# Modulation rows summed four at a time, 32 partitions each, from one accumulator tile

## The reference

```
silu_c, silu_cc = silu(c), silu(c_ctx)
for i in range(2):                                    # first block
    m  = (silu_c  @ w_mod[i] + b_mod[i]).reshape(9, 1024)    # w_mod[i]: 1024 x 9216
    mc = (silu_cc @ w_mod[i] + b_mod[i])                     # layer 0 only
    x = x + 0.5 * m[2] * swiglu(rms_norm(x) * (1 + m[1]) + m[0]);  cs likewise with mc
    x = x + m[5] * mixer(rms_norm(x) * (1 + m[4]) + m[3])
    x = x + 0.5 * m[8] * swiglu(rms_norm(x) * (1 + m[7]) + m[6])
for i in range(2):                                    # second block, conditioned on c_2
    mod = (silu(c_2) @ ada_w[i] + ada_b[i]).reshape(6, 1024)
    ...                                               # mixer and 16 experts, modulated by mod
```

## Time and profile before

| | us |
|---|---|
| median of 3 runs | 2507.69 |
| lowest and highest run | 2500.26, 2511.84 |
| the profiled execution | 2501.64 |
| its span, first to last instruction | 2499.8 |
| PE busy (share) | 2397.4 (96%) |
| DVE busy | 1430.5 (57%) |
| ACT busy | 1000.5 (40%) |
| DMA: bytes, mean rate | 535.45 MB, 214 GB/s |

### The profile page before, as it was taken

One profiled execution on the slowest core, in us unless ns is written; L12 is line 12 of the kernel. 1 busy time (PEld: TensorE's weight loads), 2 busy tenths in 40 slices (PEclk: granted clock), 3 DMA queues, 4 the chain that ended last, 5 costly groups with the idle time before them and its releaser, 6 DMA issues.

```text
span 2499.8 us, 35746 instructions
## 1 busy us (share of the span) xinstructions
PE 2397.4 (96%) x15358; PEld 2158.7 (86%) x15358; DVE 1430.5 (57%) x1609; ACT 1000.5 (40%) x1257; POOL 4.5 (0%) x12
## 2 busy tenths in 40 slices
PE   9999999989999999999999988899999899899997
PEld 7788888867998999888998986899998888899996
DVE  0875676323763465234652442688887433888886
ACT  2211132214330332042321323577776344676774
POOL 0000000000000000000000000000000000000000
PEclk8999999989999999999999988899999789899998
DMA  7456767522777477543775431488886332488884
GB/s 277 172 196 240 265 227 271 192 68 79 259 279 277 171 292 294 186 152 129 262 276 212 151 118 37 148 300 294 300 305 242 142 121 75 179 304 295 296 307 180
DMA packets 94195, 535.45 MB, mean 214 GB/s; under 512 B 9984, under 2 KB 12296, under 8 KB 46800
## 3 DMA queue, kind: packets, MB, share of 16 engines
q1 hardware_dynamic: 92480, 524.33, 58.3%
q0 software_dynamic: 816, 5.65, 0.6%
q10 hardware_dynamic: 736, 3.10, 0.3%
HBM read 531.97 MB, written 1.06 MB: 213 GB/s over the span
## 4 chain that ended last, share of the span: by engine, by line
PE 90%; DVE 6%; ACT 3%; issue 1%; DVEq 0%; ACTq 0%
PE PS L777 25%; PE PS L1231 12%; PE PS L850 9%; PE PS L888 8%; PE PS L1259 7%; PE PS L812 5%; PE PS L935 5%; DVE moe_low L2202 2%; PE PS L1199 2%; PE PS L733 2%; PE PS L699 2%; PE PS L1179 1%; PE PS L659 1%; PE PS L742 1%; PE PS L876 1%
## 5 line engine op out<-in xcount | busy, mean ns | idle before, releaser
L777 PE MATMUL PS<-h_parts,ring_low 128*128 128x256 f32 (+1 forms) x1408 | 440.0, 313 | 0.0
L777 PE MATMUL PS<-h_parts,g_parts 128*128 128x256 f32 x2112 | 383.0, 284 | 0.9 <-DVE h_parts L1813 0.9
L2202 DVE TENSOR_TENSOR moe_low<-moe_ring,W_HIGH 128x2048 fp32r<-128x2048 f32 x128 | 292.9, 2290 | 83.1 <-ACT W_HIGH L1615 83.1
L777 PEld LDWEIGHTS PS<-h_parts,g_parts 128*128 128x128 f32 x2112 | 328.9, 192 | 2.4 <-issue 1.2
L1231 PE MATMUL PS<-moe_low,HXH 128*96 128x256 f32 x1024 | 287.9, 281 | 0.0
L777 PEld LDWEIGHTS PS<-h_parts,ring_low 128*128 128x128 f32 x1408 | 269.9, 192 | 16.1
L1615 ACT ACTIVATE W_HIGH<-moe_ring 128x2048 fp32r<-128x2048 f32 x128 | 244.5, 1912 | 23.4 <-PE PS L1259 22.7
L850 PE MATMUL PS<-G,ring 128*128 128x256 f32 x1056 | 236.5, 385 | 2.8 <-DVE G L1898 2.8
L850 PEld LDWEIGHTS PS<-G,ring 128*128 128x128 f32 x1056 | 201.3, 192 | 30.7 <-DVE G L1898 3.4
L1460 ACT ACTIVATE SG<-PS 128x256 f32<-128x256 f32 (+1 forms) x88 | 38.4, 437 | 462.9 <-PE PS L777 462.9
L1231 PEld LDWEIGHTS PS<-moe_low,HXH 128*96 128x96 f32 x1024 | 166.2, 162 | 0.3
(11 more groups left out here) (316 smaller groups left out, 4653.6 us busy)
## 6 DMA issues: line engine op xcount, KB each, us to landing
moe_ring<-moe_w SPq DMA_DIRECT2D x192, 1024.0 KB, 4.9
CB<-mod_rows SPq DMA_DIRECT2D x200, 512.0 KB, 5.9
ring<-up_w SPq DMA_DIRECT2D x88, 1024.0 KB, 5.0
ring<-lin_w SPq DMA_DIRECT2D x55, 1024.0 KB, 4.9
ring<-down_w SPq DMA_DIRECT2D x24, 1408.0 KB, 6.0
CB<-mod_dual SPq DMA_DIRECT2D x24, 512.0 KB, 4.1
ring<-down_w SPq DMA_DIRECT2D x10, 1024.0 KB, 7.8
ring<-mod_w SPq DMA_DIRECT2D x8, 1024.0 KB, 7.0
```

Of the source, the lines that this page charges most:

```text
L777: return mm(dst(h), a[:, k, h * P:(h + 1) * P], b[:, k, :], start=start, stop=(k == KT - 1 and j == 2), skip_group_check=True)
L2202: tt(by_tile(moe_low[:, moe_slot(l, p), :]), by_tile(moe_ring[:, moe_slot(l, p), :]), w_high_tiles(p), ALU.subtract).then_inc(w_low, 1)
```

## The change

The sums of four rows are made from one accumulator. A **group** is four consecutive rows (7 groups for 28 rows). Each row keeps 32 of the accumulator's partitions: chunk m of a group (m = 0 to 31) holds, of each of its four rows, the 32 contraction indices m*32 to m*32 + 31, so 4 x 32 partitions by 1024 outputs, 512 KB as before. The number of chunks stays at 224, and so do DVE's instructions for a chunk, but the doubled ones are 32 now instead of 24, since the first group has four rows. The moving tile of the sums becomes a 128 x 4 table of ones and zeros (`block`), so each product gives four columns, written 8 columns apart in PSUM.

`chunk_in` issues one load a chunk whose source is `[4 rows][32 indices][1024]`, the rows 4 MB apart in DRAM; for the first group two loads, `[3][32][1024]` into 96 partitions and `[1][32][1024]` into 32. There is one accumulator for groups 1 to 6, in roots. The table of chunks, the banks and the waits (`rows_taken`, `mods_ready`) follow the groups. The conditions must be laid out by 32 partitions: POOL loads them with four small loads at the start, ACT waits for these (`ld_cond`) and takes one silu of 128 x 128. The host's data is the same. The diff, cut to its core:

```diff
+ROWS, PARTS = 4, 32
+GROUP_CHUNKS = KT * P // PARTS
+N_GROUPS = (N_DUAL + N_ROWS) // ROWS
+def group_cond(g):
+    return 0 if g < 4 else 2
 CHUNKS_AT = (
-    ([3] * 8 + [4] * 9 + [3] * 4 + [0], [4] * 5 + [2] + [4, 2] + [4] * 3 + [0]),
-    ([1, 1, 2] * 6 + [1, 1, 0, 0], [3, 2, 3, 2, 2, 2, 0, 0]),
-    ([1, 1, 2] * 6 + [1, 1, 0, 0], [3, 2, 3, 2, 2, 2, 0, 0]),
-    ([1] * 20 + [0, 0], [2] * 6 + [0, 0]),
+    ([3] * 10 + [2] + [4] * 8 + [0, 4, 0], [4] * 5 + [2, 4, 2, 0, 4, 4, 0]),
+    ([1, 1, 2] * 6 + [0, 1, 1, 0], [3, 3, 2, 2, 2, 2, 0, 0]),
+    ([2, 1] * 5 + [1, 0] + [1, 2] * 4 + [1, 0], [2] * 5 + [1, 0, 0]),
+    ([1] * 8 + [0] + [1, 2] * 6 + [0], [3, 3, 2, 2, 2, 2, 0, 0]),
 )
+GROUP_BANK = (6, 4, 7) + (4,) * (N_GROUPS - 3)
...
-                if n % KT == KT - 1:
-                    r, at = n // KT - N_DUAL, min(i + 1, len(counts) - 2)
...
+                if n % GROUP_CHUNKS == GROUP_CHUNKS - 1:
+                    steps[i + 1]["sums"].append(n // GROUP_CHUNKS)
+                    steps[i + 2]["takes"].append(n // GROUP_CHUNKS)
...
+def rows_landed(n):
+    return 16 * (n // 4 + 1 + min(n // 4 + 1, GROUP_CHUNKS // 4))
...
+    t["block"] = (i[:, None] // PARTS == np.arange(8)[None, :])
...
             def chunk_in(n):
-                src = mod_dual[n] if n < N_DUAL_CHUNKS else mod_rows[n - N_DUAL_CHUNKS]
+                g, k, part = n // GROUP_CHUNKS, n % GROUP_CHUNKS // ROWS, slice(n % ROWS * PARTS, (n % ROWS + 1) * PARTS)
                 if n >= 4:
                     sp.wait_ge(acc_steps, steps_after(n - 4))
-                sp.dma_start(ROWS_W[:, n % 4, :], src).then_inc(rows_full[n % 4], 16)
+                def put(j, rows, src):
+                    dst = ROWS_W[j * PARTS:(j + rows) * PARTS, n % 4, :]
+                    sp.dma_start(dst, src).then_inc(rows_full[n % 4], 16)
+                if g == 0:
+                    put(0, N_DUAL, mod_dual[k::KT, part, :])
+                    put(N_DUAL, 1, mod_rows[k:k + 1, part, :])
+                else:
+                    r0 = ROWS * (g - 1) + 1
+                    put(0, ROWS, mod_rows[r0 * KT + k:(r0 + ROWS - 1) * KT + k + 1:KT, part, :])
...
-            def column_sums(r):
-                pe.wait_ge(acc_steps, steps_after((N_DUAL + r + 1) * KT - 1))
...
-                for d in range(KT):
-                    last = mm(PS[:, ROW_BANK[r], d:d + 1], ACC[ROW_ACC[r]][:, d * P:(d + 1) * P], tab("ones")[:, 0:1],
-                              start=True, stop=True)
+            def column_sums(g):
+                pe.wait_ge(acc_steps, steps_after((g + 1) * GROUP_CHUNKS - 1))
+                wait(pe, rows_taken, g)
+                for j in range(1 if g else 2):
+                    acc = ACC if g else DUAL_ACC[:, j, :]
+                    for d in range(KT):
+                        at = j * ROWS * KT + d
+                        last = mm(PS[:, GROUP_BANK[g], at:at + 3 * KT + 1:KT], acc[:, d * P:(d + 1) * P],
+                                  tab("block")[:, 0:ROWS], start=True, stop=True)
                 last.then_inc(colsum_done, 1)
-            def dual_column_sums(r):
...
@@ down0 on PE
-                            pe.wait_ge(rows_taken, 11)
+                            pe.wait_ge(rows_taken, 3)
...
@@ ACT at the start
+            act.wait_ge(ld_cond, 64)
+            af(cond_rows[:, :, :], cond_raw[:, :, :], ACT.Silu).then_inc(cond_ready, 1)
...
@@ POOL at the start
+            for part in range(ROWS):
+                src = bass.AP(cols_in.tensor, part * PARTS * NCOLS, [[0, ROWS], [NCOLS, PARTS], [1, 4 * KT]])
+                pool.dma_start(cond_raw[:, part, :], src).then_inc(ld_cond, 16)
...
             def add_chunk(n):
+                g, m = n // GROUP_CHUNKS, n % GROUP_CHUNKS
+                dve.wait_ge(rows_full[n % 4], rows_landed(n))
+                for j in range(1 if g else 2):
+                    acc = ACC if g else DUAL_ACC[:, j, :]
+                    at = 4 * (m // ROWS) + (group_cond(g) if g else j)
+                    c = cond_rows[:, m % ROWS, at:at + 1]
+                    if m == 0:
+                        if g > 1:
+                            dve.wait_ge(colsum_done, g)
+                        ts(acc, w, c, None, ALU.mult).then_inc(acc_steps, 1)
+                    else:
+                        dve.wait_ge(acc_steps, steps_after(n - 1) if g else 2 * n - 1 + j)
+                        stt(out=acc, in0=w, scalar=c, in1=acc, op0=ALU.mult, op1=ALU.add).then_inc(acc_steps, 1)
```

More of the change, by code:

```diff
@@ L84, in chunk_plan @@
         counts = list(ups_at) + list(downs_at)
-        steps = [dict(chunks=[], sums=[], dual=[], takes=[]) for _ in counts]
+        steps = [dict(chunks=[], sums=[], takes=[]) for _ in counts]
         for i, count in enumerate(counts):
@@ L88, in chunk_plan @@
                 steps[i]["chunks"].append(n)
-                if n % KT == KT - 1:
-                    r, at = n // KT - N_DUAL, min(i + 1, len(counts) - 2)
-                    if r < 0:
-                        steps[at]["dual"].append(r + N_DUAL)
-                    else:
-                        steps[at]["sums"].append(r)
-                        steps[min(at + 1, len(counts) - 1)]["takes"].append(r)
+                if n % GROUP_CHUNKS == GROUP_CHUNKS - 1:
+                    steps[i + 1]["sums"].append(n // GROUP_CHUNKS)
+                    steps[i + 2]["takes"].append(n // GROUP_CHUNKS)
                 n += 1
         plan.append(steps)
-    assert n == (N_DUAL + N_ROWS) * KT
+    assert n == N_GROUPS * GROUP_CHUNKS
     return plan
@@ L157 @@
 _TABS = (("ident", P), ("flip", P), ("mean64", P), ("mean128", P), ("mean1024", P), ("rot_axial", P),
[L158 removed]
+         ("rot_half", P), ("upper", P), ("ones", P), ("zeros", P), ("w4", 8), ("w16", 32), ("iota", CAP), ("block", 8),
          ("cos_axial", S), ("sin_axial", S), ("cos_half", S), ("sin_half", S),
@@ L690, in first_mods @@
                 spread_roots(0)
[L692 to L711 removed]
+            def column_sums(g):
[7 more added lines that the diff above has]
+                                  tab("block")[:, 0:ROWS], start=True, stop=True)
+                last.then_inc(colsum_done, 1)
             def sums(f, i):
[L715 to L718 removed]
+                for g in PLAN[f][i]["sums"]:
+                    column_sums(g)
             def h_arrived(n, k):
@@ L1870, in add_chunk @@
-                r, k = q // KT, q % KT
-                c, acc = cond_flat[:, q:q + 1], ACC[ROW_ACC[r]]
-                if k == 0:
-                    wait(dve, colsum_done, max([0] + [o + 1 for o in range(r) if ROW_ACC[o] == ROW_ACC[r]]))
-                    ts(acc, w, c, None, ALU.mult).then_inc(acc_steps, 1)
-                else:
-                    dve.wait_ge(acc_steps, steps_after(n - 1))
-                    stt(out=acc, in0=w, scalar=c, in1=acc, op0=ALU.mult, op1=ALU.add).then_inc(acc_steps, 1)
@@ new lines, in take_group @@
+            def take_group(g):
+                dve.wait_ge(colsum_done, g + 1)
+                at = ROW_TILE0 + (g * ROWS - N_DUAL) * KT
+                bias = COL["mod_b"].start + at
+                if g == 0:
+                    line(tt(M[:, at:at + N_DUAL * KT, 1], PS[:, GROUP_BANK[0], ROWS * KT:(ROWS + N_DUAL) * KT],
+                            cols[:, bias:bias + N_DUAL * KT], ALU.add))
+                tt(M[:, at:at + ROWS * KT, 0], PS[:, GROUP_BANK[g], 0:ROWS * KT], cols[:, bias:bias + ROWS * KT], ALU.add)\
+                    .then_inc(rows_taken, 1)
+                dve.wait_ge(rows_taken, g + 1)
+                line.wait()
@@ L1898, in up @@
                     tt(G[:, i, 0:N], SG[:, i % 4, 0:N], src, ALU.mult).then_inc(g_ready, 1)
-                    for r in step["takes"]:
-                        take_row(r)
+                    for g in step["takes"]:
+                        take_group(g)
                     for n in step["chunks"]:
```

83 lines of the change are left out of this document (17 added, 66 removed).

## The result

| | before | after |
|---|---|---|
| median (runs), us | 2507.15 (4) | 3133.05 (4) |
| lowest and highest run | 2500.26, 2511.84 | 3126.78, 3138.48 |
| ratio, with its 95% interval | | 1.2498 [1.2459, 1.2538] |
| profiled execution; its span | 2501.64; 2499.8 | 3126.78; 3125.0 |
| granted PE clock, mean | 0.958 | 0.873 |

The account below looks back on a forecast made before the run. PE bounds the kernel before; 38.6 + 5 - 3, about 41 us, would be gained, but chunk loads on few engines make the ffns +190, +64, +60, +65: +379 on 2501.6, about 2885 us, range 2790 to 3110.

Parts of the forecast that it names:

- Passes removed: PE's sums of modulation rows: 368 passes fewer at 0.105 us, 38.6 us gained, four moved columns costing nothing extra.
- Slow stretches: PE's slower products after some sums, in the first up stage and the down stages: 5 us gained, bounds 0 and 6.
- Loads dealt out by outermost count: SyncE's chunk loads: the outermost count, not bytes, sets the engines used, so 4 a chunk, 3 for the 96-partition piece.
- the same engines each time: Chunk loads: assumed always on the same 4 engines; with a turning choice a load would only land 3.8 us later.
- A chunk at 5.02 us: A 512 KB chunk on 4 engines: 128 KB on each at 26.1 GB/s takes 5.02 us.
- A unit of 1024 KB is 2.51 us of every engine, one of 1408 KB 3.45: Weight loads between the chunks: their price on each engine, added to the chunks' time in every ffn.
- The bound of 23.5 GB/s: Slower engines, 298 GB/s at share 0.79: 11% more than the 1,460 us of engine time, giving 3050 us.
- Spread as before: Rival: chunk loads still use 16 engines, so the removed passes pay, 2467 us; chance 0.12.
- Nothing in sum: Rival: loads spread, but passes priced by moved columns, so the 38.6 us gain goes, 2506 us; chance 0.03.
- Landing "well over 10": Sign of few engines: a chunk's time to landing rises from 4 to 6 us to well over 10.
- A DMA share under 0.5 in the up stages: Sign of few engines: the DMA engines' busy share in the up stages falls under 0.5 while PE waits.
- DMA queues hold up one another: Named example of being wrong in size alone: steps long, but not by engine time.

Follow-up runs that it names:

- e2_packed: The kernel after, but the host packs each chunk into one block of 128 rows, one load a chunk; 2449.14 us, ratio 0.9774 to before.
- e3_k4_near: e2_packed with a spare row behind every 32, so outermost count 4 with blocks 132 KB apart; 3115.21 us, ratio 1.2432.
- e5_before_k4: The kernel before, changed only in storing chunks as 4 blocks of 32 rows and a spare (outermost count 4); 3161.00 us, ratio 1.2615.
- e8_interleaved: The kernel after with the load's source turned to 32 indices outermost, four rows inside, on the host's old data; 2446.40 us, ratio 0.9778.

## Why the prediction was right, and where it failed

**Passes removed, 38.6 us, and four columns at no price: right.** 16 passes with four columns take 1.68 us in e2_packed. In after PE waits in all four ffns, as forecast. That the savings vanish there is not borne out: with every chunk at count 4 the new sums and plan are still 46 us faster than the old (3115.21 against 3161.00), two executions each.

**Slow stretches, 5 us: too small.** The two versions with whole loads gain 57 and 58 us where 41 was forecast. The last unit's 12.98 went to 11.05 as hoped, but the products of 512 columns also started every 0.2267 us in place of 0.2333, 0.3 us less a unit in ffn 0, for which the sum had no term.

**Loads dealt out by outermost count: right**, and the step that decided. The eight-row load's 88 packets were enough to see it; the 2,208 packets of after, the share of 0.26, and e3_k4_near, e5_before_k4 and e8_interleaved show it. So was "the same engines each time", for which no row of before spoke; of the runs' evidence for it, the busy share of 0.26 with four chunks under way is the plainest.

**A chunk at 5.02 us: right**, 5.10 measured.

**"A unit of 1024 KB is 2.51 us of every engine, one of 1408 KB 3.45": the step that failed.** It was taken from stretches in which all loads are spread alike. Beside chunks on few engines the unit takes 3.9 to 4.4 us and the larger one 4.95, in the kernel's first up stage 25.0 - 4 x 5.10 = 4.6. With 4.0 for a unit this step is worth some 180 of the 248 us by which the trace exceeds the forecast: 30 x 1.5 = 45 in the first ffn, 22 x 1.5 + 8 x 1.5 = 45 in each of the others. The smaller error is the first group's chunk, 5.33 forecast, 5.87 measured. The bound of 23.5 GB/s was meant to cover slower engines; in the mixture a busy engine moves 18 on average, so the range's end of 3110 was too low by 23 us for a cause that it did not hold.

With the measured prices (4.0 for a unit, picked from the lower half of 3.9 to 4.4) the forecast's own sum gives the last chunk of ffn 0 at 52.3 + 6 + 32 x 5.87 + 72 x 5.10 + 30 x 4.0 = 733 us; the chain has it at 713.07 + 23.48 = 736.6, forecast 666. In a later ffn 40 x 5.10 + 22 x 4.0 + 8 x 4.95 = 332 us, less the same 15 us of loads issued ahead, put the last chunk at start + 317; the chain has 1213.6 - 891.7 = 322, 1544.3 - 1233.9 = 310 and 1995.4 - 1673.1 = 322, forecast 267 to 270. So the loads explain 67 + 3 x 49 = 214 of the 248 us between forecast and trace; this depends on the price picked, as 4.4 would give 745 and start + 325. Another 23 us lie behind the last chunk: 20, 30 and 24 us in the later ffns instead of 17, because one or two down units were still to come, the first of them in 12.25 to 12.53 us and not 9.6, at a granted clock of 0.76 to 0.80 behind PE's wait. Some 11 us are not attributed.

**The rivals.** *Spread as before* fell for after, but e2_packed and e8_interleaved are its case: its 2467 us was 18 to 21 us too high. For four loads of 32 rows, expected at the same 2467, it was 33 us too low. *Nothing in sum* fell with the 1.68 us.

**What was named as a sign.** Landing "well over 10": 21.4 us for a unit. Steps of 18 to 23 us: 25, and in the later up stages 31.5 us for three (983.09 to 1014.65 on the chain), 10.5 each and not 9. A DMA share under 0.5 in the up stages: 0.4 in the first, but 0.55 to 0.62 in the later ones, and this miss was the hint at the unit's price, as the engines are busy for longer than their bytes need. "DMA queues hold up one another" had been named as what would make the size wrong. It came close, but SP's queue held both kinds of load, so it was not queues against each other.

## What to carry to other kernels

Before a load is given a source in blocks, look at the outermost count, not at the bytes: on SyncE's queue 512 KB took 1.36 us with 128 rows outermost, 5.10 with 4 and 10.15 with 2, and turning two dimensions round, with the partitions renumbered and the 0/1 table to match, brought 1.38 from the same DRAM. Price a mixture of loads from a mixture: the other loads of the queue, dealt out over all 16 engines, cost 1.4 to 1.7 times their own time beside loads on a few. And where a change rearranges work for one engine's sake, do the rearranged load and the saved work as separate runs: here the one brought -58 us and the other +684 us on top of it, or +654 us by itself in the old kernel.

## What the runs showed of the hardware that had not been expected

- Where loads on all 16 engines and loads on four are under way together, a busy engine moves 18 GB/s on average instead of 25 to 26 (170 GB/s at a share of 0.59, against 423 at 1.01 and 105 at 0.26). The packets slow down, and on engines without a chunk too: 69% of the units' packets take over 350 ns, where none does with units alone. Cause open.
- Some forms of load have slow packets on the same number of engines: count 8 with 17 rows of 4 KB between block starts takes 4.26 us a chunk (266 ns a packet of 4 KB), with 24 rows 2.60 (159 ns), with 4 MB 2.66; count 16 with 9 rows 2.24 (275 ns), where the loads of 128 and of 32 x 4 rows take 1.36 and 1.38 (163 ns). Count 4 showed no such thing at 33 rows (5.12 against 5.10). A small distance is not the only form: four loads of 32 rows, each of one block, take 2.31 us (283 ns). Which partitions are written at the same time differs between these forms as well, and no run varied that by itself. Cause open.
- A float32 product with four moved columns takes what one with one column takes, 0.105 us a pass.
- Products of 512 columns started every 0.233 us in the two kernels with the old sums and plan and every 0.227 in the seven with the new ones, at the full granted clock and already before the first sum of the stage. Cause open.
